# Root mean square applied behind the products, first MLP panel split during the output projection, attention weights copied one unit behind

## The reference, cut to what matters

```python
def _layernorm(x, g, b, eps=1e-5):          # last step of the first block: ln2_g, ln2_b of layer 1
    return (x - mean(x)) * rsqrt(var(x) + eps) * g + b

def rmsnorm(x, g):
    return x * rsqrt(mean(x * x) + 1e-6) * g

for layer in range(2):
    h = rmsnorm(x, attn_norm[layer])
    mem_kv = rmsnorm(mem, mem_norm[layer]) @ w_mem_kv[layer]
    if layer == 0:
        q, kc, vc, ks, vs, kw, vw, q_mem, gl = split(h @ a_w_in)
        o = concat([nsa_attention(...), memory_attention(q_mem, mem_kv)])    # 12 heads, compressed keys too
        x = x + o @ a_w_out
    else:
        k_s, v_s = split(rmsnorm(x, kv_norm) @ w_kv_shared)
        q, q_mem = split(h @ b_w_in)
        o = concat([dilated_attention(...), memory_attention(q_mem, mem_kv)])  # 3 patterns, 8 heads
        x = x + o @ b_w_out
    hm = rmsnorm(x, mlp_norm[layer])
    x = x + square(relu(hm @ w_up[layer])) @ w_down[layer]      # 1024 -> 4096 -> 1024
return x
```

## Time and profile before

| | us |
|---|---|
| median of 3 runs | 2546.41 (2545.17 to 2547.43) |
| the profiled execution | 2540.58 |
| its span | 2538.8 |

### The profile page before, as it was taken

One profiled execution on the slowest core, in us unless ns is written; L12 is line 12 of the kernel. 1 busy time (PEld: TensorE's weight loads), 2 busy tenths in 40 slices (PEclk: granted clock), 3 DMA queues, 4 the chain that ended last, 5 costly groups with the idle time before them and its releaser, 6 DMA issues. The chain is left out here.

```text
span 2538.8 us, 42804 instructions
## 1 busy us (share of the span) xinstructions
PE 2395.5 (94%) x17534; PEld 2124.7 (84%) x17534; DVE 1729.7 (68%) x1891; ACT 954.9 (38%) x1148; POOL 6.4 (0%) x14
## 2 busy tenths in 40 slices
PE   7999989979999999999999999999977998997998
PEld 6999679968998688999989999997764997875997
DVE  4774277757762488888988879884553776554776
ACT  4423010034341276776766667662251000132000
POOL 0000000000000000000000000000000000000000
PEclk9999999989999999999999999999977999988999
DMA  5232345533323488988989889874402554311554
GB/s 196 101 117 84 133 151 188 188 112 107 117 101 117 166 304 320 347 335 323 358 317 348 335 327 339 333 296 148 149 1 69 180 184 164 133 50 51 181 182 149
DMA packets 68603, 495.17 MB, mean 195 GB/s; under 512 B 7584, under 2 KB 7712, under 8 KB 9104
## 3 DMA queue, kind: packets, MB, share of 16 engines
q1 hardware_dynamic: 67072, 485.57, 52.0%
q0 software_dynamic: 1424, 8.04, 0.8%
HBM read 492.54 MB, written 1.05 MB: 194 GB/s over the span
## 5 line engine op out<-in xcount | busy, mean ns | idle before, releaser
L336 PE MATMUL wide<-ring_hi,xe_hi 128*128 128x256 f32 x1088 | 313.9, 288 | 7.1 <-DVE ring_more_lo L2443 7.1
L1070 PE MATMUL wide<-ring_hi,xe_lo 128*128 128x256 f32 x1088 | 306.5, 282 | 0.0
L336 PE MATMUL wide<-ring_hi,hT_hi 128*128 128x512 f32 x664 | 260.9, 393 | 2.6 <-DVE ring_lo L2522 2.6
L336 PE MATMUL wide<-xT_hi,ring_hi 128*128 128x256 f32 x864 | 244.7, 283 | 17.9 <-DVE ring_lo L2522 16.5
L1070 PE MATMUL wide<-ring_hi,hT_lo 128*128 128x512 f32 x664 | 261.1, 393 | 0.0
L1070 PE MATMUL wide<-xT_hi,ring_lo 128*128 128x256 f32 x864 | 249.7, 289 | 0.0
L2443 DVE TENSOR_TENSOR ring_more_lo<-ring_more,ring_hi 128x2048 fp32r<-128x2048 f32 x96 | 219.3, 2291 | 41.0 <-ACT ring_hi L1752 40.1
L1069 PE MATMUL wide<-xT_lo,ring_hi 128*128 128x256 f32 x864 | 246.7, 286 | 0.0
L2443 DVE TENSOR_TENSOR ring_lo<-ring,ring_hi 128x2048 fp32r<-128x2048 f32 x96 | 220.1, 2293 | 34.9 <-ACT ring_hi L1752 33.5
L336 PE MATMUL wide<-mix_xT_hi,mix_hi 128*128 128x256 f32 x768 | 229.7, 299 | 5.1 <-DVE xT_lo L2026 5.1
L2522 DVE TENSOR_TENSOR ring_lo<-ring,ring_hi 128x2048 fp32r<-128x2048 f32 x96 | 220.1, 2292 | 3.3
(11 more groups left out here) (458 smaller groups left out, 5134.4 us busy)
## 6 DMA issues: line engine op xcount, KB each, us to landing
ring<-in_weights SPq DMA_DIRECT2D x316, 1024.0 KB, 4.8
ring_more<-in_weights SPq DMA_DIRECT2D x120, 1024.0 KB, 4.8
xT<-in_weights SPq DMA_DIRECT2D x24, 1024.0 KB, 4.8
ln_row<-in_ln_rows POOLq DMA_DIRECT2D x4, 1024.0 KB, 6.8
x_tm<-in_x SPq DMA_DIRECT2D x1, 1024.0 KB, 5.8
qkT<-in_mem POOLq DMA_DIRECT2D x1, 1024.0 KB, 5.1
out<-x_tm SPq DMA_DIRECT2D x1, 1024.0 KB, 4.0
cst<-in_consts SPq DMA_DIRECT2D x1, 1009.5 KB, 11.7
```

What stands on the lines that cost most here:

```text
L336: ins = self.pe.matmul(out, lhsT, rhs, start=start, stop=stop)
L1070: return pe.matmul(out, lhsT[1], rhs[0], start=False, stop=stop)
```

## The change

**Root mean square.** `rms` and `rms_x` are gone, and so is `xn`. TensorE transposes `x_tm` itself. Ahead of attention the inverse root (`inv_rms`) is a scale that ScalarE applies when it copies a projection out of PSUM (in `copy_tokens`, two instructions of 128x256 in place of one of 128x512). Behind the MLP the square of it (`inv_ms`) is a factor in the last addition, since relu and square let a positive factor through as its square. The sums of squares are made by ScalarE behind its copies (`squares`, `root`), no longer ahead of the transposes.

**Last layer norm.** TensorE transposes the normalized x while its gain and bias are not on yet; `copy_xT` puts them on together with the attention's gain (`both_g`, `both_b`, made once by two 128x8 products at the start of the experts). `ln_gain` follows behind. The two products for the memory's keys and values stand on either side of the transposes.

**First MLP panel.** VectorE splits it after the copies of `o_tm`'s transposes, before it waits for the output projection.

**Attention units.** ScalarE copies the weights one unit behind (`turned(n - 1)`), VectorE finishes four units behind (`finish(n - 4)`), and `compress_weights` comes after the second unit's maxima instead of the first's.

```diff
@@ attention_pe
-                    project_tokens(MEM_PANELS, MEM_PANELS, memT[1])
-                pe.wait_ge(S["rms_x"], 2 * l + 1)
-                turn_x(n_turn, xn)
+                    project_tokens(1, MEM_PANELS, memT[1])
+                    pe.wait_ge(S["ln_z"], 2 * DEPTH)
+                    turn_x(n_turn, x_tm)
+                    project_tokens(1, MEM_PANELS + 1, memT[1])
+                else:
+                    pe.wait_ge(S["y_read_2"], 1)
+                    turn_x(n_turn, x_tm)
...
-                pe.wait_ge(S["rms_x"], 2 * l + 2)
+                pe.wait_ge(S["x_done"], l + 1)
                 wait_xT(n_turn)
-                turn_x(n_turn + 1, xn)
+                turn_x(n_turn + 1, x_tm)
@@ scalar engine
+            def squares():
+                for tt in range(TT):
+                    ins = act.activation(o_tm[:, tt, :], x_tm[:, tt, :], ACT.Square, accum_out=rs[:, tt:tt + 1])
+                return ins
+            def root(l):
+                if l == 0:
                     act.wait_ge(S["ln_x_done"], 2 * DEPTH)
+                squares().then_inc(S["act_step"], 1)
...
+                if dst is proj:
+                    act.wait_ge(S["rms_x"], l + 1)
+                    for tt in range(TT):
+                        ins = act.activation(dst[:, tt, j * PC:(j + 1) * PC], b[:, tt * PC:(tt + 1) * PC], ACT.Copy, scale=inv_rms[:, tt:tt + 1])
...
-                for n in range(n_units + 2):
+                for n in range(n_units + 1):
                     if n < n_units:
                         exps(n0 + n)
-                    if n >= 2:
-                        turned(n0 + n - 2)
+                    if n >= 1:
+                        turned(n0 + n - 1)
@@ attention_act
-                    rms(0, x_tm)
-                    for j in range(MEM_PANELS):
-                        copy_tokens(0, mem_kv[:, 1], MEM_PANELS + j, j)
-                    copy_xT(n_turn, "attn_norm0")
+                    copy_tokens(0, mem_kv[:, 1], MEM_PANELS, 0)
+                    copy_xT(n_turn, "both_g", "both_b")
+                    copy_tokens(0, mem_kv[:, 1], MEM_PANELS + 1, 1)
+                    root(0)
...
-                    rms(2, x_tm)
                     copy_xT(n_turn, "kv_norm")
                     copy_xT(n_turn + 1, "attn_norm1", dst=xT2)
+                    root(1)
...
-                rms(2 * l + 1, x_tm)
                 split_xT(n_turn + 1, xT_hi, f"mlp_norm{l}")
+                squares().then_inc(S["rms_std"], 1)
@@ vector engine
+                for f in ("g", "b"):      # at the start of moe_dve
+                    tt_(col[:, COLS[f"both_{f}"]], col[:, COLS[f"ln2_{f}1"]], col[:, COLS["attn_norm0"]], ALU.mult)
...
-                        ins = stt(xs, xs, ALPHA if gated else 1.0, bank[4 + 2 * tt + h][:], ALU.mult, ALU.add)
+                        b = bank[4 + 2 * tt + h][:]
+                        ins = stt(xs, xs, ALPHA, b, ALU.mult, ALU.add) if gated else stt(xs, b, inv_ms[:, tt:tt + 1], xs, ALU.mult, ALU.add)
...
+            def inverse_rms(l):
+                dve.wait_ge(S["rms_std"], 2 * l + 1)
+                dve.reciprocal(inv_rms, rs[:, 2:2 + TT]).then_inc(S["rms_x"], 1)
...
-                for n in range(n_units + 3):
+                for n in range(n_units + 4):
                     if n < n_units:
                         maxima(n0 + n)
-                    if l == 0 and n == 0:
+                    if l == 0 and n == 1:
                         compress_weights()
-                    if n >= 3:
-                        finish(n0 + n - 3)
+                    if n >= 4:
+                        finish(n0 + n - 4)
...
                 copy_xT(n_turn)
+                n = ORDER.index(("mlp_up", l, 0)) - AFTER_MOE
+                split_first(n, landed_2, (BEFORE_MOE + n) % RING, PER_ITEM + 2 * l * (D_FF_2 // FCH))
                 dve.wait_ge(S["proj2_mm"], l + 1)
...
-                rms_x(2 * l + 1, x_tm)
                 split_xT(n_turn + 1, xT_hi, f"mlp_norm{l}")
@@ end of the first block
                     layer_norm(2 * l + 1, acc)
+                    copy_xT(2 * l + 2, "both_g", "both_b")
                     ln_gain(2 * l + 1)
```

More of the change, by code:

```diff
@@ L496, in program @@
         attn = ExitStack()
-        xn = sb("xn", TT, D, stack=attn)
+        sb("spare", TT, D, stack=attn)
         proj = sb("proj", TT, 11 * PC, stack=attn)
@@ L612, in values @@
             return proj[:, k, a:a + HEAD]
+        inv_rms, inv_ms = rs[:, 88:88 + TT], rs[:, 90:90 + TT]
         def turned_at(n):
@@ L1817, in copy_tokens @@
                 act.wait_ge(S["attn_proj"], l * PANELS_ATTN[0] + n + 1)
-                act.activation(dst[:, :, j * PC:(j + 1) * PC], bank[4 + (l * PANELS_ATTN[0] + n) % 2][:].rearrange("p (t c) -> p t c", t=TT),
-                               ACT.Copy).then_inc(S["attn_read"], 1)
+                b = bank[4 + (l * PANELS_ATTN[0] + n) % 2]
+                if dst is proj:
+                    act.wait_ge(S["rms_x"], l + 1)
+                    for tt in range(TT):
+                        ins = act.activation(dst[:, tt, j * PC:(j + 1) * PC], b[:, tt * PC:(tt + 1) * PC], ACT.Copy, scale=inv_rms[:, tt:tt + 1])
+                else:
+                    ins = act.activation(dst[:, :, j * PC:(j + 1) * PC], b[:].rearrange("p (t c) -> p t c", t=TT), ACT.Copy)
+                ins.then_inc(S["attn_read"], 1)
                 act.wait_ge(S["attn_read"], made.next("attn_read"))
@@ L1961, in attention_act @@
                 copy_xT(n_turn)
-                rms(2 * l + 1, x_tm)
                 split_xT(n_turn + 1, xT_hi, f"mlp_norm{l}")
+                squares().then_inc(S["rms_std"], 1)
+                act.wait_ge(S["rms_std"], made.next("rms_std"))
                 mlp_act("mlp", D_FF_2 // FCH, l * (D_FF_2 // FCH), 3)
@@ L2511, in mlp_dve @@
                 first_slot = 0 if gated else BEFORE_MOE
-                done = [1 if gated else 0]
+                done = [1]
                 def split_panel(turn=0, per_turn=0):
@@ L2561, in mlp_dve @@
                     lower_in(1, 1)
+                else:
+                    inverse_square(l)
                 dve.wait_ge(sems["y"], base + n_chunks)
@@ L2565, in mlp_dve, with inverse_square @@
                         xs = x_tm[:, tt, h * 512:(h + 1) * 512]
-                        ins = stt(xs, xs, ALPHA if gated else 1.0, bank[4 + 2 * tt + h][:], ALU.mult, ALU.add)
+                        b = bank[4 + 2 * tt + h][:]
+                        ins = stt(xs, xs, ALPHA, b, ALU.mult, ALU.add) if gated else stt(xs, b, inv_ms[:, tt:tt + 1], xs, ALU.mult, ALU.add)
                 ins.then_inc(sems["read"], 1)
                 dve.wait_ge(sems["read"], 1 + l)
-            def rms_x(n, src):
-                dve.wait_ge(S["rms_std"], n + 1)
-                if n:
-                    dve.wait_ge(S["x_turned"], 4 * (4, 5, 7, 8)[n])
-                dve.reciprocal(rs[:, 4:4 + TT], rs[:, 2:2 + TT]).then_inc(S["dve_step"], 1)
+            def inverse_rms(l):
+                dve.wait_ge(S["rms_std"], 2 * l + 1)
+                dve.reciprocal(inv_rms, rs[:, 2:2 + TT]).then_inc(S["rms_x"], 1)
+                dve.wait_ge(S["rms_x"], made.next("rms_x"))
+            def inverse_square(l):
+                dve.wait_ge(S["rms_std"], 2 * l + 2)
+                ts_(inv_ms, rs[:, 0:TT], 1.0 / D, RMS_EPS, ALU.mult, ALU.add).then_inc(S["dve_step"], 1)
                 dve.wait_ge(S["dve_step"], made.next("dve_step"))
-                for tt in range(TT):
-                    ins = ts_(xn[:, tt, :], src[:, tt, :], rs[:, 4 + tt:5 + tt], None, ALU.mult)
-                ins.then_inc(S["rms_x"], 1)
-                dve.wait_ge(S["rms_x"], made.next("rms_x"))
+                dve.reciprocal(inv_ms, inv_ms).then_inc(S["dve_step"], 1)
+                dve.wait_ge(S["dve_step"], made.next("dve_step"))
             def rotate(dst1, dst2, src, n, cos, sin, parts=slice(0, P)):
@@ L2813, in attention_dve @@
                 dve.wait_ge(S["params_in"], 16 * 5)
-                rms_x(2 * l, x_tm)
                 if l == 0:
-                    copy_xT(n_turn, "attn_norm0")
                     norm_heads(0, 0)
+                    inverse_rms(0)
                     norm_heads(0, 1)
@@ L2835, in attention_dve @@
                     copy_xT(n_turn + 1, "attn_norm1", dst=xT2)
+                    inverse_rms(1)
                     dve.memset(o_tm[:, :, (SLOTS + MEM_HEADS) * HEAD:], 0.0).then_inc(S["dve_step"], 1)
```

23 lines of the change are left out of this document (6 added, 17 removed).

## The result

The changed kernel takes 2475.51 us (median of 4 runs, 2474.28 to 2476.50) against 2545.80 (4 runs, 2545.17 to 2547.43): a ratio of 0.9713, interval 0.9694 to 0.9731, or 70 us less. The forecast was 2491, with a range of 2473 to 2510. The profiled executions, 2474.79 against 2540.58, differ by 65.8; the forecast for that pair was 55.7.

The account below looks back on a forecast made before the run. TensorE was taken to bound the MLP loops, so gains lay in its waits and its lowered clock in attention. Terms 26.6 + 3.7 + 7.6 + 15 + 4 - 1.2 = 55.7 us off 2546.4 gave 2491 us, range 2473 to 2510.

Parts of the forecast that it names:

- the forecast's own 0.70: Whole kernel: chance given to the forecast itself, with its own range of 2478 to 2500 us.
- MLP starts, 26.6: Start of both MLPs: root chain off the path, first panel split early; 11.6 to 15.2 us each, 13.3 taken, 26.6 together.
- The second panel: MLP starts: ready 9.8 us after the transposes' start, just when TensorE wants it; no wait or a few tenths.
- the drain would give 2.8 us more: Two ScalarE table loads leaving the path: 2.8 us more by the skill page's drain figure; left out of the sum.
- Hand-overs, 3.7 and 7.6: Hand-overs to layers 0 and 1: TensorE's waits go; 3.7 us (2.6 to 3.7) and 7.6 (lower bound 4.4).
- Attention, 15 and 4: Attention units: earlier copies remove waits for pT_sb; layer 0 gains 15 us (8 to 21), layer 1 gains 4 (0 to 7).
- On top of it the clock: Layer 0's attention units: fewer half-clock stretches on TensorE add 4 us, between 0 and 10, to the 11 from waits.
- Costs, 1.2: Split projection copies 0.6 us, two small products before the experts 0.3, second panel a few tenths: 1.2 us lost.
- The clock did come along: Rival, chance 0.14: half-clock stretches stay wherever TensorE paused; gain only 42 us, time 2504.
- TensorE's waits for exponentials: Attention rival, chance 0.08: copies wait for transposes, exponentials start late, neither attention stage gains; gain 37 us, time 2510.
- the split was hidden: MLP-start rival, chance 0.04: first panel lands late, its split is not hidden; 3.5 us a start come back, time 2498.
- the series of one unit after another: Slower rival, chance 0.03: attention units run each in series, 2.3 us more on 25 units; time 2566.

Follow-up runs that it names:

- filler: The kernel before, attention order untouched, with 8 more 128x128 TensorE products ahead of the transposes of each unit with scores of its own: 2557.70 us, ratio 1.0048.
- compress_first: The changed kernel with the compressed weights' softmax in layer 0 after the first unit's maxima again: 2487.09 us, one run.
- split_only: The kernel before with only the first panel's split of each MLP moved ahead of VectorE's wait for the output projection: 2528.14 us, ratio 0.9921.
- copies_two_behind: The changed kernel with ScalarE's copies of the attention weights two units behind again: 2502.79 us.
- finish_three_behind: The changed kernel with VectorE's finish three units behind again, copies one unit behind as changed: 2478.64 us.

## Where the prediction was right, and the step that failed

The measured 2475.5 us lies below 2478, where the forecast's own 0.70 began. The waits that were to go went, as forecast; one term of the sum, the clock in the attention units, was several times too small.

**MLP starts, 26.6: right.** 14.1 and 13.5 were measured. The direct parts came as counted: 5.67 from the chain of the root in each layer (36.80 to 31.13 us ahead of the transposes in layer 0), where the rows had given 5.65, 6.1 and 6.7 from there to the first product. The clock gave back 2.4 and 1.2 of the first up product, inside the 0 to 2.8. The full clock did not hold through: either the transposes or the product lost time to it. That this came out near the middle value in both layers was not derived; the prediction took the middle of two rows. The second panel made no wait. The Trainium skill (ScalarE: Activation LUTs, "What ACT_TABLE_LOAD costs") adds a drain of 1.38 us to a switch of tables. The trace doesn't agree: the root starts 0.02 us behind the load. The prediction's remark that the drain would give 2.8 us more was wrong besides, since a drain would already be part of the 5.65 us between the two rows.

**Hand-overs, 3.7 and 7.6: right for layer 0, right by luck for layer 1.** Layer 0 gave 4.05, a little over its upper bound. The inverse root came at 1752.4, not 1750, and still in time. Layer 1 gave 7.1 with its projections. The 4.4 us between the addition and the transposes went, though the addition itself is 0.25 longer. But the transposes stayed at the lower clock (3.33 us against 3.68) and gave 0.35 instead of 1.7. The difference was made up by 1.3 us that the prediction had at nothing, from the MLP's loop: there a chunk takes 11.21 us instead of 11.31 (the mean from the fourth `gate_s` to the sixteenth). The figure repeats in all 14 profiles and in both layers: 11.31 to 11.32 in the five without the new root mean square and layer norm, 11.21 in the nine with them. Why the loop is faster stays open.

**Attention, 15 and 4: the mechanism right, the clock's term much too small.** The step of the prediction that failed is "On top of it the clock [...] I count 4, between 0 and 10". The direct term was 11 and measured 10.9. The clock's was 12.6, over the upper bound; the 81 us became 57.8, below the 60 given as the lowest. The working had 21 us as the worth of the whole lower clock and took a fifth, since "the first of them stays". (The 21 took in TensorE's idle time; over the 64 us of its busy time the same sum gives 17.) That first wait did stay (2.59 us), but TensorE was back at the full clock within 5 us of it, with no second wait in between. `filler` and `compress_first` show the tie between waits and clock that the prediction only weighed. With 11 of the 13.6 us of waits gone, most of the 17 would have come nearer than a fifth of the 21. In layer 1 the clock's term was 5.3, not 3. There the cause is not shown: with the old order those units took 60.2 and 60.3 us in the kernel before, but 54.1 in `split_only` and in `copies_two_behind`, with the same wait of about 1 us for `pT_sb`. The new order was at 52.0 to 53.4. So 1 to 2 us are the order's own, and some 6 come and go without it. What decides that stays open.

**Costs, 1.2: not what was counted.** The wait for the last copy ahead of the attention units, for which 0.6 stood, grew by 0.2 us in layer 1 (1.17 against 0.94) and by nothing in layer 0. The projections of layer 0 took 1.95 longer all the same, of which 1.8 is one stretch of compressed scores that fell on the lower clock (4.99 us against 3.21); in `finish_three_behind` it took 2.86. The end came 1.2 sooner, which I had not counted: it is the faster loop again.

**The base.** Forecast and result differ by 15.2 us: 10.1 in the pair of profiled executions, where attention alone gave 8.5 and 2.9 more than forecast, and 5.1 because the profiled execution before lay 5.8 below its median and the one after only 0.7. I had subtracted the gain from both alike. Of the 8.4 us by which the second block of the kernel before differs in its two profiles, 5.1 lie in the attention units of layer 0, which repeat to 0.1 us in the changed one.

**Rivals.** The clock did come along; TensorE's waits for exponentials stayed at the 2.6 and 4.3 us of before; the split was hidden; the series of one unit after another did not form.

## What to carry to other kernels

Where TensorE's granted clock is below 1 in a stage full of short waits, split its busy time by the clock before pricing a change: removing the waits gave back both here, 10.9 us of idle time and 12.6 by the clock. Look first at waits that follow closely on another one while the clock is still low, as in `compress_first`, and move small work off that path even if the engine that does it has slack. Scale factors that commute with a product, and splits of weights that have landed, can stand behind or ahead of a hand-over: out of it they were worth 13 and 14.5 us at the two MLP starts.

## What was not expected of the hardware

- Five VectorE instructions of 1.9 us, moved one unit earlier, cost 9.4 us, 8.5 of them as TensorE at 1.2 GHz.
- 23.7 us of added products left a stage at 78.5 us that took 81.3 and 86.4 without them.
- The MLP's loop ran at 11.21 us a chunk in all nine profiles with the new root mean square and layer norm, and at 11.31 to 11.32 in the five without.
- The same 403 TensorE instructions were busy for 51.0 us in the changed kernel, 63.6 in the kernel before and 72.9 in its second profile.
- A product of 128x128 by the identity in f32 is two instructions, 0.25 us, where a transpose of the same size is one of about 0.12.
